# Cached keys and cached values of the loop issued from ScalarE's queue instead of SyncE's

## The reference, cut to what matters

```
k_past = cache_k[page_table].reshape(DB, P, N_HEADS, HEAD_DIM)   # DB = 8, P = 4096: 32 pages of 128 for each
v_past = cache_v[page_table].reshape(DB, P, N_HEADS, HEAD_DIM)
...
s = jnp.einsum('bqhd,bkhd->bhqk', q, k_all) * HEAD_DIM ** -0.5
s = s + (Fh[..., P:, None] - Fh[..., None, :])
p = jax.nn.softmax(s, axis=-1)
out = jnp.einsum('bhqk,bkhd->bqhd', p, v_all)
```

## Time and profile before

| | us |
|---|---|
| median of 3 runs | 1354.66 |
| time of the profiled execution | 1352.25 |
| its span | 1350.2 |
| PE busy | 1309.5 (97%) |
| ACT busy | 401.2 (30%) |
| POOL busy | 603.6 (45%) |
| DVE busy | 664.8 (49%) |
| mean granted clock of TensorE | 0.993 |

### The profile page before, as it was taken

The page is one execution under the profiler, slowest core; times in us unless marked ns, Lnnn a source line. Parts: engine busy times, 40 slices in busy tenths (PEclk is TensorE's granted clock), DMA queues, the critical chain, the costliest instruction groups (busy, mean ns, idle before and its releaser), DMA issues. The chain is left out here.

```text
span 1350.2 us, 21210 instructions
## 1 busy us (share of the span) xinstructions
PE 1309.5 (97%) x7595; PEld 1047.7 (78%) x7595; DVE 664.8 (49%) x1013; ACT 401.2 (30%) x589; POOL 603.6 (45%) x287
## 2 busy tenths in 40 slices
PE   8899999999899999999999999999999999999996
PEld 7888898988799976777777777677777776667675
DVE  4744555534576654636456473645544134311327
ACT  4546666664521341120212111111211202111016
POOL 1017787843400257565765655676662112021114
PEclk9999999999999999999999999999999999999999
DMA  7335454420254157777687877778684534567633
GB/s 234 116 123 163 152 173 142 140 90 9 79 186 161 36 174 247 253 262 240 225 267 225 273 233 248 232 242 266 204 282 157 203 126 174 196 260 278 228 132 125
DMA packets 111769, 255.02 MB, mean 189 GB/s; under 512 B 12848, under 2 KB 22961, under 8 KB 106280
## 3 DMA queue, kind: packets, MB, share of 16 engines
q1 hardware_dynamic: 102384, 247.00, 54.4%
q10 hardware_dynamic: 8320, 4.19, 1.1%
q0 software_dynamic: 960, 2.47, 0.5%
HBM read 243.73 MB, written 10.12 MB: 188 GB/s over the span
## 5 line engine op out<-in xcount | busy, mean ns | idle before, releaser
L887 POOL TENSOR_TENSOR WL<-WR,WH 128x1024 fp32r<-128x1024 f32 x55 | 132.0, 2401 | 352.3 <-ACT WH L1125 352.3
L795 POOL TENSOR_TENSOR AR<-AR,QB 128x1024 f32<-128x1024 f32 x96 | 232.6, 2440 | 89.8 <-DMA AR<-cache_k 77.3
L1552 PE MATMUL PSM<-XH,WH 128*128 128x512 f32 x672 | 213.9, 400 | 0.0
L1552 PE MATMUL PSM<-XL,WH 128*128 128x512 f32 x672 | 208.2, 391 | 0.0
L1552 PE MATMUL PSM<-XH,WL 128*128 128x512 f32 x672 | 207.5, 390 | 0.0
L2131 DVE TENSOR_TENSOR ACC<-ACC,PSM 128x512 f32<-128x512 f32 x160 | 108.5, 684 | 142.4 <-PE PSM L1562 142.2
L1125 ACT CAST WH<-WR 128x1024 fp32r<-128x1024 f32 x55 | 57.5, 1047 | 364.8 <-PE PSM L1552 185.9
L1552 PEld LDWEIGHTS PSM<-XH,WH 128*128 128x128 f32 x672 | 122.0, 188 | 50.5 <-issue 27.6
L1562 PE MATMUL PSM<-R 128*128 128x512 f32 x528 | 148.5, 391 | 0.1
L1552 PEld LDWEIGHTS PSM<-XL,WH 128*128 128x128 f32 x672 | 126.2, 188 | 27.5
L1552 PEld LDWEIGHTS PSM<-XH,WL 128*128 128x128 f32 x672 | 126.2, 188 | 27.4
(11 more groups left out here) (275 smaller groups left out, 2198.4 us busy)
## 6 DMA issues: line engine op xcount, KB each, us to landing
AR<-cache_v SPq DMA_DIRECT2D x256, 256.0 KB, 3.3
AR<-cache_k SPq DMA_DIRECT2D x192, 256.0 KB, 3.5
AR<-ws SPq DMA_DIRECT2D x37, 1024.0 KB, 6.4
WR<-ffn SPq DMA_DIRECT2D x66, 512.0 KB, 4.9
WR<-w_in SPq DMA_DIRECT2D x20, 512.0 KB, 4.6
ACC<-cache_k SPq DMA_DIRECT2D x32, 256.0 KB, 2.9
WR<-cache_k SPq DMA_DIRECT2D x32, 256.0 KB, 3.1
WR<-w_o SPq DMA_DIRECT2D x5, 1024.0 KB, 5.1
```

The costliest lines, as they stand in the source:

```text
L795: pool.tensor_tensor(keys, keys, QB[:].rearrange("p (o n) -> p o n", o=1).to_broadcast([P, KP, AW]), ALU.mult).then_inc(k_mul, 1)
L887: pool.tensor_tensor(lo, WR[:, raw_weight(e), :], hi.bitcast(F32), ALU.subtract).then_inc(ffn_lo, 1)
L1552: ins = pe.matmul(out[:, hc], (hi, lo)[a][:, k * P:(k + 1) * P], x[b][:, k, hc], start=(k == 0 and n == 0), stop=(k == KC - 1 and n == 2))
```

## The change

Value pages and key tiles of the loop are issued from ScalarE's instruction stream. A value page stands in each of the 8 units after a value unit (`VPAGE`), with its own register load just ahead of it; the first page of a chunk waits for the chunk's buffer. A key tile (two register loads, a wait, two DMAs) stands in the same unit as before, behind ScalarE's other work of that unit. The first three key tiles and the first two value chunks stay with SyncE, ahead of the loop, as do weights, factors and the sample rows' weight stream.

```diff
--- before.py
+++ after.py
@@ -134,7 +134,8 @@
 
 SPREAD, SUBTRACT, EXPONENT, SUM, DENOM, INVERT = 1, 2, 3, 5, 11, 12
 VALUES = (9, 21, 32, 43)
-VLOAD = tuple(o + n for o in VALUES for n in (1, 2))
+VPAGE = {b * WIN + o + 1 + n: (b * NCH + 2 * i + 2 + n // CH, n % CH) for b in range(NB) for i, o in enumerate(VALUES)
+         for n in range(2 * CH) if b * NCH + 2 * i + 2 < NB * NCH}
 SUBTRACT0, EXPONENT0, SUM0 = 6, 8, 9
 OWN, COLUMNS, MAXIMUM, KEEP, HEADMAX = WIN - 5, WIN - 3, WIN - 2, WIN - 2, WIN - 1
 LATE = NB * NKP - EARLY
@@ -611,10 +612,7 @@
 
             def keys(n):
 
-                if n >= KS:
-                    pages(EARLY + n, KR, n % KS, t["cache_k"], k_ld, k_red, EARLY + n - KS + 1)
-                else:
-                    pages(EARLY + n, KR, n, t["cache_k"], k_ld)
+                pages(EARLY + n, KR, n, t["cache_k"], k_ld)
 
             def weight_tile(e):
                 kind, f, _ = WORDER[e]
@@ -689,7 +687,7 @@
                     stream_tile(0)
                 if u == (NB - 1) * WIN + SUBTRACT + 3:
                     stream_tile(1)
-                if u == (NB - 1) * WIN + VLOAD[-1]:
+                if u == (NB - 1) * WIN + VALUES[-1] + 2:
                     stream_tile(2)
                     sp.wait_ge(v_used, NB * NCH)
                     sp.dma_start(xs1, t["xs"]).then_inc(e_ld, 16)
@@ -714,13 +712,6 @@
                     sp.dma_start(svec, t["ln2_b"].to_broadcast([NB, D])).then_inc(e_vec_ld, 16)
                 if b >= NB:
                     continue
-                for n in range(KS, LATE):
-                    if u == KRED[n - KS] + 1:
-                        keys(n)
-                for c in range(2, NCH + 2):
-                    n = b * NCH + c
-                    if o == VLOAD[c - 2] and n < NB * NCH:
-                        pages(n, VR, n % 2, t["cache_v"], v_ld, v_used, n - 1)
                 for n in range(NE + 1, NB):
                     if u == Q_LOAD[n - NE - 1]:
                         queries(n)
@@ -1217,6 +1208,23 @@
                 sums = PSM[:, 7, 0:2 * NB * tiles].rearrange("p (a b) -> p a b", b=2 * NB)
                 act.activation(hsilu[:, 0:tiles, :], sums[:, :, 0:NB], ACT.Silu).then_inc(e_silu, 1)
 
+            def key_pages(n):
+
+                numbers = [act.value_load(page[0:1, bass.ds((EARLY + n) * KP + j, 1)], min_val=0, max_val=POOL_PAGES - 1)
+                           for j in range(KP)]
+                act.wait_ge(k_red, EARLY + n - KS + 1)
+                for j, p in enumerate(numbers):
+                    act.dma_start(KR[n % KS][:, j * AW:(j + 1) * AW],
+                                  t["cache_k"][bass.ds(p, 1), :, :].rearrange("a p n -> (a p) n")).then_inc(k_ld[n % KS], 16)
+
+            def value_page(n, j):
+
+                p = act.value_load(page[0:1, bass.ds(n * CH + j, 1)], min_val=0, max_val=POOL_PAGES - 1)
+                if j == 0:
+                    act.wait_ge(v_used, n - 1)
+                act.dma_start(VR[n % 2][:, j * AW:(j + 1) * AW],
+                              t["cache_v"][bass.ds(p, 1), :, :].rearrange("a p n -> (a p) n")).then_inc(v_ld[n % 2], 16)
+
             for u in range(LAST):
                 b, o = divmod(u, WIN)
                 if u in TURN_U:
@@ -1234,6 +1242,11 @@
                         hidden_hi(f)
                 if b < NB and o == (EXPONENT if b else EXPONENT0):
                     exponentials(b)
+                if u in VPAGE:
+                    value_page(*VPAGE[u])
+                for n in range(KS, LATE):
+                    if u == KRED[n - KS] + 1:
+                        key_pages(n)
                 if u == NORM2 - 1:
                     factors()
                 if u >= NORM2 and u % 2 == 0 and (u - NORM2) // 2 <= RT:
```

## The result

The changed kernel takes 1388.51 us (median of 4 runs, 1387.94 to 1390.44) against 1352.68 us for the kernel before (4 runs): ratio 1.0276, 95% interval 1.0244 to 1.0308. The profiled execution has a span of 1385.9 us against 1350.2. So it is slower by 36 us; the forecast was +24 us on the profiled execution, 1378 in all.

A forecast was written before the change was run, and what follows sets the result against it. TensorE bounds the loop, with 4.2 us of waits to win. Late value pages 20, first interval 3, key waits 4, less 3.4 us of old stalls: +23.6 on 1352.25, 1375.9; median 1378, range 1354 to 1418 us.

The forecast's parts named there:

- What bounds the loop: TensorE's own pace, busy 595.4 of 600 us; its 4.2 us of waits, 0.3%, are the ceiling of a gain.
- Price of a page: Queue time to look up and issue one page on ScalarE, taken from SyncE's row: 1.07 us.
- Overlap: ScalarE queue work begins when the compute ahead starts; a single cast costs the queue 0.1 us, a pair 1.0 us.
- rival 3: On ScalarE, register loads wait till the compute in front has ended: +51 to +65, 1405 to 1420 us; chance 0.15.
- rival 2: On ScalarE, register loads run ahead while it waits: total +13, 1368 us; chance 0.15.
- The walk: Interval 589.05 to 606.11: 12 pages, 12.8 us on ScalarE's queue; TensorE stands 1.5 to 2.3 us for the last.
- the main term: Late value pages in nine of 13 fully loaded 17.1 us intervals, about 2.2 us each: 20 us.
- What stays hidden: Casts and SiLU up to 5 us late cost nothing; slack 8.5 us, beyond which one for one.
- Key waits: On ScalarE, waits for reductions that free key buffers hold what stands behind: a tenth of 43 us, 4 us.
- rival 4: ScalarE, VectorE and GpSimd wait in a circle; half of the 43 us come through: +41, 1396 us; chance 0.14.
- Landing: A page lands 2.5 to 3.3 us after its DMA instruction begins.

The follow-up runs named there:

- the two kernels that take them away: Against the kernel before: values on ScalarE two to a unit, keys on SyncE, 0.998; keys alone on ScalarE, value chunks whole on SyncE, 0.9985 in 12 runs.
- three kernels: Values spread on ScalarE, keys on SyncE, 1.0066; values spread on SyncE, keys on ScalarE, 1.0068; changed kernel without page lookup on ScalarE, 1.0092.
- The kernel with the lowest ratio: Against the kernel before: value pages on ScalarE two to a unit (o+1 to o+4), keys on SyncE; 1348.90 us, ratio 0.998.

## Why the prediction was right, and where its sizes were off

- **What bounds the loop.** Right: nothing was to be won but the 0.3% of TensorE's waits, and the two kernels that take them away gain 0.1 to 0.2%, of which only one is clear of no change (0.998).
- **Price of a page.** 1.05 us (3.48 us for four DMA instructions with three register loads between: (3.48 - 0.34)/3), forecast 1.07. A register load on ScalarE is 0.287 us (SyncE: 0.264):

```profile
L1222 ACTq TENSOR_LOAD <-PG x1: 287/287/287, 599.4 to 599.4; - x1
```

- **Overlap.** Mostly right. The loads start at 599.4, with the SiLU, not after it, which refutes rival 3. Nor do they run ahead of a waiting SiLU: from the end of the key DMAs at 594.04 to 599.33 the queue did nothing but a table load, though the next page's load needed only the page table. This place alone doesn't say what held it, for the cast behind the SiLU has a wait of its own for the same matmuls (`act.wait_ge(g_full, f)`), and the queue is through it at 599.3 too. The exponential at 913.91 has nothing of the kind behind it; it waited 0.89 us for VectorE, and the register load of a key tile behind it starts with it and not before:

```profile
L1109 ACTq EVENT_SEMAPHORE  x1: 17/17/17, 599.3 to 599.3; - x1
...
911.74 1.28 ACT L1162 ACT_TABLE_LOAD   x1 [5.24 <-issue]
913.91 0.42 ACT L1162 ACTIVATE PR<-PR 128x256 f32<-128x256 f32 x1 [0.89 <-DVE lsub L2089]
...
L1213 ACTq TENSOR_LOAD <-PG x1: 292/292/292, 913.9 to 913.9; - x1
```

  That refutes rival 2, and the trace doesn't bear out the reading of the Trainium skill ("Perfetto Trace Analysis", the DVE / Act engine instruction) on which it was built. But the prediction's own rule, that queue work begins when the instruction ahead starts, is not quite right either. An instruction whose semaphores are there and which only waits for its engine holds nothing up: the load of 599.4 stands behind the cast of 600.25 in the program and runs before it. So a cast behind a SiLU costs the queue nothing, where I took 1.0 us for the pair.
- **The walk.** 12 pages, 12.9 us, late in the interval walked by about 1 us of idle time, forecast 1.5 to 2.3. The next unit's 6.68 us was forecast as 1.8 to 2.6. The sum of waits, 32.9 us, was forecast as 27 (20 + 3 + 4). By the interval that ends with them (value units found in TensorE's order of time), the waits were 20.6 us for the intervals that had been 17.1 us, forecast 20, and nothing for those of 26.3 us, as forecast. So the main term was right in sum, with luck in it, since one stall of 6.68 us is a third. The intervals of 18.9 us were mis-sized: the first one cost 5.5 us, forecast 3, and the others, which were to just fit, 6.7 us.
- **What stays hidden.** Right: TensorE has no wait for silu, lo parts or hidden values here, with casts some 4 us late. Whole chunks on ScalarE show the end of that slack.
- **Key waits and rival 4.** Too small as well: I took 4 us of a possible 43. The waits grew to some 60 us, and about 12 of 33 us of stalls went when they were moved away. Those 12 are part of the stalls counted above, not beside them. Rival 4's circle (late cast, late reduction, late key) is in the trace at 614 to 620, through VectorE's own order. But SyncE in the same order loses as much, so ScalarE's part in the circle isn't needed for a loss of this size.
- **Landing.** I took 2.5 to 3.3 us from the earlier trace rows. The page that TensorE waited for at 596.64 was 5.0 us under way:

```profile
L1225 ACTq DMA_DIRECT2D AR<-cache_v x1: 344/344/344, 591.6 to 591.6; - x1
...
DMA to landing us min/median/max: 5.0/5.0/5.0
```

The page behind the 6.68 us stall was asked for at 633.93, 2.9 us after its value unit began, and was 4.8 us under way. The median of all pages is 3.3 us as before. A stall can fall on a slow page, and a page asked for in time hides that. I take this for what is left where the queue isn't full (5.6, 10.2 and 14.5 us of waits in three kernels); it was not followed page by page there.
- **Busy time.** Not foreseen, and the largest miss: 7.8 us, most of it the clock (see below). With 5.9 us more of waits than forecast and 1.6 us less in the rest of the program, it makes up the 12 us between +24 and +36.
- **The attribution.** The prediction walked the right queue, but its title and its rivals spoke of ScalarE's load; that the same order costs the same on SyncE was in the arithmetic (1.07 us was SyncE's own price) and I didn't draw it. Stated as "ScalarE is too full" it would have been wrong. The three costs are not additive, since each late page gives the next one time.

Open: how the 10 us of waits that spreading alone costs divide between place and DMA traffic. Values asked for two to a unit land no sooner (4.3 us) and leave 0.7 us of waits, so the late place is needed for it; it wasn't tried with the weight tiles taken out.

## What to carry to other kernels

When a transfer moves to another queue, list what stands ahead of the *last* piece that a consumer waits for: pieces x price + the waits between them + the landing of a slow transfer, against the time until it is read. Spreading issues evenly to be kind to the issuing engine puts the last piece latest of all; here two a unit cost 0.3%, one a unit 2.8%. Split a change into its queue and its order before naming one as the cause.

## What the runs showed of the hardware

A stall costs more than its length. After the 6.7 us stall that ended at 638.7, TensorE's granted clock is 0.50 (1.2 GHz) in place of 1.00 (2.4 GHz); it had fallen before the stall's end (0.88 over the first window). The windows of the changed kernel over the stall and behind it:

```profile
631.00:638.70 7.70, 1.05 (x9) 0.12 (x8) 1.81 (x2) 0.00 (x0) 7.65 (x4) 0.88 0.80 277
638.70:643.00 4.30, 4.27 (x12) 1.06 (x13) 0.00 (x0) 0.00 (x0) 3.37 (x2) 0.50 0.86 265
643.00:650.00 7.00, 7.00 (x35) 5.86 (x34) 4.36 (x6) 0.00 (x0) 0.35 (x1) 0.95 0.05 8
```

12 matmuls in 4.3 us, 35 in the next 7.0. It happened at three stalls in all of this stretch, those in the value units of 508, 631 and 705 us, and never in the kernel before. The stall at 705 was 3.01 us, and one of the same 3.01 us at 792 did not bring it, so length alone doesn't settle it. TensorE's row at the end of each, and the window behind it:

```profile
708.80 1.89 PE L1624 MATMUL PSM<-AR,PR 128*8 128x512 f32 x8 [3.01 <-DMA AR<-cache_v]
708.80:713.00 4.20, 4.20 (x16) 2.06 (x17) 0.00 (x0) 0.00 (x0) 0.00 (x0) 0.62 0.77 249
...
795.67 1.04 PE L1624 MATMUL PSM<-AR,PR 128*8 128x512 f32 x8 [3.01 <-DMA AR<-cache_v]
795.60:800.00 4.40, 4.33 (x23) 2.88 (x24) 0.00 (x0) 0.28 (x1) 1.16 (x1) 1.00 0.11 39
```

Behind the three stalls some 11 us went by at half clock (from the clock shares of the windows: 4.3 and 0.7 us here, 3.2 us of the window from 708.80, and 3.0 us behind the stall at 508). Half of that, some 5.6 us, is an estimate of what the clock cost; the other 2 us of the 7.8 us of busy time are not accounted for. With the order on SyncE the clock fell five times, which is why that kernel loses as much with less waiting for cache_v:

```profile
481.43:1148.54 667.11, 638.33 (x3006) 468.08 (x3004) 313.35 (x366) 112.05 (x119) 358.02 (x146) 0.98 0.70 220
```

Idle 28.8 us and busy 638.3, against 34.2 and 633.0 in the changed kernel for the same work: 667 us both.

Loads of keys and values from two queues side by side land later than from one: medians of 4.0 and 4.1 us with values on ScalarE and keys on SyncE (3.9 and 3.8 us the other way round), 3.3 and 3.4 us before, 3.3 and 3.1 us in the changed kernel. The kernel with the lowest ratio has it too (values 4.3 us, at the same 233 GB/s in all from 480 to 1110 us as the kernel before) and loses nothing by it; it asks for its last page four units earlier than the spread order does.
